# Layer 1's adaLN weights in 24 groups of eight blocks, with slots of their own

## What is computed

```python
cs = jax.nn.silu(c)
for i in range(DEPTH):
    mod = cs @ ada_w[i] + ada_b[i]                      # (9 rows) x 2048 x 12288
    sh1, sc1, g1, sh2, sc2, g2 = jnp.split(mod, N_ADA, axis=-1)
    h = rmsnorm(x, norm_mix_g[i]) * (1.0 + sc1[:, None]) + sh1[:, None]
    ...                                                 # layer 0: retention, layer 1: pooling mixer
    x = x + g1[:, None] * out
    h = rmsnorm(x, norm_ffn_g[i]) * (1.0 + sc2[:, None]) + sh2[:, None]
    x = x + g2[:, None] * swiglu(h, ffn_w_in[i], ffn_w_out[i])
```

## Time and profile before

| | |
|---|---|
| median of three runs | 3528.49 us (3526.47 to 3534.52) |
| the profiled execution, its own time | 3536.41 us |
| its span (first to last instruction) | 3534.6 us |
| TensorE busy | 3344.4 us, 95% |
| weight loads into TensorE (overlap the matmuls) | 3085.7 us, 87% |
| VectorE busy | 1757.5 us, 50% |
| ScalarE busy | 1096.7 us, 31% |
| moved by DMA | 701 MB, mean 198 GB/s |
| mean granted TensorE clock | 0.965 of 2.4 GHz |
| first feed-forward, first weight block to the last output lap | 1363 to 2396 us |
| layer 1's first feed-forward step | 2546 to 2618 us |

### The profile page before, as it was taken

The page is one execution under the profiler, slowest core; times in us unless marked ns, Lnnn a source line. Parts: engine busy times, 40 slices in busy tenths (PEclk is TensorE's granted clock), DMA queues, the critical chain, the costliest instruction groups (busy, mean ns, idle before and its releaser), DMA issues.

```text
span 3534.6 us, 54959 instructions
## 1 busy us (share of the span) xinstructions
PE 3344.4 (95%) x23769; PEld 3085.7 (87%) x23769; DVE 1757.5 (50%) x2696; ACT 1096.7 (31%) x1356; POOL 95.0 (3%) x149
## 2 busy tenths in 40 slices
PE   7799999999999987999999999996699999999997
PEld 3598888988889867999999999996599999999997
DVE  3134473645636475444444444446835555555555
ACT  2232222323223223333332323233333333333333
POOL 0000000000000010000000000001100000000000
PEclk7799999999999998999999999997799999999998
DMA  9775868668686765667666666662264444444442
GB/s 314 250 241 192 273 200 257 211 218 259 205 265 207 226 212 180 219 226 227 226 222 218 217 215 216 219 218 94 74 212 149 150 150 150 151 151 151 149 149 72
DMA packets 627858, 701.12 MB, mean 198 GB/s; under 512 B 21133, under 2 KB 590925, under 8 KB 627289
## 3 DMA queue, kind: packets, MB, share of 16 engines
q1 hardware_dynamic: 606016, 619.26, 54.5%
q0 software_dynamic: 20512, 74.97, 6.6%
q10 hardware_dynamic: 1090, 3.38, 0.3%
HBM read 656.05 MB, written 41.48 MB: 197 GB/s over the span
## 4 chain that ended last, share of the span: by engine, by line
PE 87%; DMA 5%; DVE 5%; ACT 1%; issue 1%; ACTq 0%; POOL 0%; SPq 0%; POOLq 0%; DVEq 0%
PE pair L1323 26%; PE pair L1325 25%; PE pair L1324 25%; PE adab L1339 4%; DMA sb_raw<-in_ada_w 3%; DVE sb_w_lo L819 1%; PE m L1309 1%; DMA sb_o_s<-in_ada_w 1%; DVE sb_silu_g L859 1%; PE m L1534 1%; PE m L1568 1%; DVE sb_big L1134 1%; PE pair L1309 1%; DMA sb_raw<-in_ret_w_in 1%; DMA sb_big<-in_ada_w 1%
## 5 line engine op out<-in xcount | busy, mean ns | idle before, releaser
L819 DVE TENSOR_TENSOR sb_w_lo<-sb_raw,sb_w_hi 128x1024 fp32r<-128x1024 f32 x792 | 965.3, 1223 | 1323.5 <-ACT sb_w_hi L540 1317.3
L540 ACT ACTIVATE sb_w_hi<-sb_raw 128x1024 fp32r<-128x1024 f32 x792 | 838.1, 1059 | 1957.4 <-PE pair L1325 1182.0
L1323 PE MATMUL pair<-sb_h_hi,sb_w_hi 128*128 128x320 f32 x4480 | 1414.6, 316 | 32.0 <-DVE sb_h_lo L1235 15.1
L1325 PE MATMUL pair<-sb_h_hi,sb_w_lo 128*128 128x320 f32 x4480 | 1393.1, 311 | 0.0
L1324 PE MATMUL pair<-sb_h_lo,sb_w_hi 128*128 128x320 f32 x4480 | 1393.0, 311 | 0.0
L1323 PEld LDWEIGHTS pair<-sb_h_hi,sb_w_hi 128*128 128x128 f32 x4480 | 849.0, 190 | 83.2 <-issue 50.0
L1324 PEld LDWEIGHTS pair<-sb_h_lo,sb_w_hi 128*128 128x128 f32 x4480 | 849.1, 190 | 0.0
L1325 PEld LDWEIGHTS pair<-sb_h_hi,sb_w_lo 128*128 128x128 f32 x4480 | 848.2, 189 | 0.0
L1323 PE MATMUL pair<-sb_y_hi,sb_w_hi 128*128 128x320 f32 x1856 | 581.5, 313 | 10.7 <-DVE sb_y_lo L1122 10.7
L1324 PE MATMUL pair<-sb_y_lo,sb_w_hi 128*128 128x320 f32 x1856 | 575.4, 310 | 0.0
L1325 PE MATMUL pair<-sb_y_hi,sb_w_lo 128*128 128x320 f32 x1856 | 575.2, 310 | 0.0
(11 more groups left out here) (212 smaller groups left out, 1489.0 us busy)
## 6 DMA issues: line engine op xcount, KB each, us to landing
sb_raw<-in_ffn_w_in SPq DMA_DIRECT2D x352, 512.0 KB, 3.6
sb_raw<-in_ada_w SPq DMA_DIRECT2D x320, 512.0 KB, 4.7
sb_raw<-in_ret_w_in SPq DMA_DIRECT2D x192, 512.0 KB, 6.0
sb_raw<-in_ffn_w_out SPq DMA_DIRECT2D x176, 512.0 KB, 3.7
sb_big<-in_state_ret POOLq DMA_DIRECT2D x32, 1024.0 KB, 8.0
sb_raw<-in_ret_w_out SPq DMA_DIRECT2D x64, 512.0 KB, 4.1
out_state_ret_sample<-sb_big POOLq DMA_DIRECT2D x32, 1024.0 KB, 5.8
sb_big<-in_ada_w SPq DMA_DIRECT2D x20, 512.0 KB, 7.2
```

Source lines behind the costliest of these rows:

```text
L540: A(w_hi[s][:, :, :], raw[slot][:, :, :], ACT.Copy).then_inc(hi_done, 1)
L819: V.tensor_tensor(w_lo[s][:, :, :], raw[slot][:, :, :], w_hi[s][:, :, :].bitcast(F32), ALU.subtract)\
L1323: MM(out, wh, hi[:, c, :], start=first and k == 0, stop=False)
L1325: ins = MM(out, wl, hi[:, c, :], start=False, stop=last and k == BK - 1)
```

## The change

Layer 1's ada blocks leave the ring. They get nine slots (`v_tok`, `o_s` and seven pieces of `big`, which lie unused during the first feed-forward) and are done in 24 groups of two strips, eight blocks each, at every eleventh weight block of the first feed-forward: group g after its weight block 11g + 6 (`ada_eight`), the fold of both strips one block later (`fold_eight`; both are called after every `gemm` of a lap), ScalarE's copy of 512 columns at its split 11g + 10, ahead of the posts (`copy_eight`), VectorE's add at its split 11g + 11, behind them (`take_eight`). The loads go out on SyncE between the weight loads, block i of group g after the load with number 11g + 4 + i (`load_ff`, `load_eight`), not before number 8 from the third block on. Block b waits for block b - 9 to be used; the third to ninth wait for `h_ready` 8 instead. Layer 1's first step has no ada work any more.

```diff
+FF_FIRST, EIGHT_FROM, EIGHT_EVERY, EIGHTS = H * 32, 6, 11, 24
+EIGHT_SLOTS = 9
...
+def eights_due(gemms, late=0):
+    g, rest = divmod(gemms - FF_FIRST - EIGHT_FROM - late, EIGHT_EVERY)
+    return rest == 0 and 0 <= g < EIGHTS
...
-    halves += [True] * 4 + ([True] * 2 + none + [True] * 2) * (FF_STEPS - 1) + none + none
-    halves += [True] * 4 + none * 3 * (FF_STEPS - 1) + none
+    halves += none * 2 * (1 + 3 * FF_STEPS)
...
+        eight = [t.rearrange("p (k n) -> p k n", k=BK) for t in
+                 [v_tok[:, :, :].rearrange("p c t -> p (c t)"), o_s[:, :, :].rearrange("p c t -> p (c t)")]
+                 + [big[:, 1024 * i:1024 * i + 1024] for i in range(EIGHT_SLOTS - 2)]]
+        eight_sb = k_tok[:, :, :].rearrange("p t n -> p (t n)")
...
+            def load_eight(b):
+                g, i = divmod(b, 8)
+                e = b % EIGHT_SLOTS
+                if b >= EIGHT_SLOTS:
+                    sp.wait_ge(ada_done, 4 * 3 * DC + b - EIGHT_SLOTS + 1)
+                elif b < 2:
+                    sp.wait_ge(pe["F"], H)
+                    sp.wait_ge(state_prompt_out, 16 * H)
+                else:
+                    sp.wait_ge(h_ready, 8)
+                sp.dma_start(eight[e], block_of(a["ada_w"][1], 512 * (i % 4), BN * (2 * g + i // 4))).then_inc(eight_in[e], 16)
+            eights = [max(EIGHT_EVERY * (b // 8) + 4 + b % 8, 8 if b >= 2 else 0) for b in range(8 * EIGHTS)]
+            def load_ff(layer, src):
+                load_block(src)
+                while layer == 0 and eights and C.n["gemm"] - FF_FIRST >= eights[0]:
+                    eights.pop(0)
+                    load_eight(8 * EIGHTS - 1 - len(eights))
...
+            def copy_eight():
+                act.wait_ge(ada_done, C("adas") * 4 + 8)
+                act.wait_ge(ada_folded, C("adas", -ADA0))
+                A(eight_sb, adab[:, :], ACT.Copy).then_inc(ada_copied, 2)
+                C.n["adas"] += 2
...
+                    if eights_due(C.n["gemm"], 4):
+                        copy_eight()
...
+            def take_eight():
+                dve.wait_ge(ada_folded, C("adas", 2 - ADA0))
+                chunk = C("adas", -3 * DC) * 2
+                bias = ada_bT[:, C("adas") * 2:C("adas") * 2 + 4].unsqueeze(2).broadcast_to([P, 4, NC9])
+                src = mbank[C("adas", 0, 2) % 2][:, 0:4 * NC9].rearrange("p (c n) -> p c n", c=4)
+                V.tensor_tensor(mods[1][:, chunk:chunk + 4, :], src, bias, ALU.add).then_inc(mod_dve, 2)
+                C.n["adas"] += 2
...
+                    if eights_due(C.n["gemm"], 5):
+                        take_eight()
...
+            def ada_eight():
+                pe_.wait_ge(ada_copied, C("adas", -ADA0))
+                for i in range(8):
+                    b = C.n["ada"] - 4 * 3 * DC
+                    e, lap = b % EIGHT_SLOTS, b // EIGHT_SLOTS
+                    pe_.wait_ge(eight_in[e], 16 * lap + 16)
+                    for j in range(4):
+                        ins = MM(adab[KPAD * j:KPAD * j + KPAD, BN * (i // 4):BN * (i // 4) + BN], csT[:, 4 * (i % 4) + j, :],
+                                 eight[e][:, j, :], start=i % 4 == 0, stop=i % 4 == 3)
+                    ins.then_inc(ada_done, 1)
+                    C.n["ada"] += 1
+                C.n["adas"] += 2
+            def fold_eight():
+                pe_.wait_ge(ada_copied, C("folds", 2 - ADA0))
+                pe_.wait_ge(mod_dve, C("folds", -2 * H))
+                bank = mbank[C("folds", 0, 2) % 2]
+                for c in range(4):
+                    ins = MM(bank[:, NC9 * c:NC9 * c + NC9], eight_sb[:, P * c:P * c + P], fold, start=True, stop=True)
+                ins.then_inc(ada_folded, 2)
+                C.n["folds"] += 2
+            def eights_beside():
+                if eights_due(C.n["gemm"]):
+                    ada_eight()
+                if eights_due(C.n["gemm"], 1):
+                    fold_eight()
```

More of the change, by code:

```diff
@@ new lines, in _, with feed_forward @@
+            eights = [max(EIGHT_EVERY * (b // 8) + 4 + b % 8, 8 if b >= 2 else 0) for b in range(8 * EIGHTS)]
+            def feed_forward(layer, i, out=True):
+                w1, w2 = a["ffn_w_in"][layer], a["ffn_w_out"][layer]
+                for col in (i * 512, None, i * 512 + DFF):
+                    if col is None and out:
+                        for s in range(8):
+                            load_ff(layer, block_of(w2, i * 512 - 512, BN * s))
+                    elif col is not None:
+                        for n in range(8):
+                            load_ff(layer, block_of(w1, 512 * (n % 4), col + BN * (n // 4)))
@@ L394, in _ @@
+            assert not eights
             for s in range(8):
                 load_block(block_of(a["pool_w"][0, s // 2], 0, BN * (s % 2)))
[L396 to L399, removed]
+            feed_forward(1, 0, out=False)
+            for i in range(1, FF_STEPS):
+                feed_forward(1, i)
             load_k4(a["ffn_w_out"][1], (FF_STEPS - 1) * 512)
@@ L787, in _ @@
             split_ahead()
-            norm(3, GAIN_FFN + DC, mods[1], SH2, ada=True)
-            feed_forward(first=True, ada=True, ahead=AHEAD, end=True)
-            copy_ada()
+            norm(3, GAIN_FFN + DC, mods[1], SH2)
+            feed_forward(first=True, ahead=AHEAD)
             for _ in range(1, FF_STEPS):
@@ L833, in take_mod, with lap @@
                 C.n["adas"] += step
-            def lap(posts, ada=False, pend=False, ahead=0, take=True):
+            def take_eight():
[5 more added lines that the diff above has]
+                C.n["adas"] += 2
+            def lap(posts, ahead=0):
                 for k in range(8):
@@ L1169, in out_between_steps @@
                 split()
-            lap({6: [finish_k]}, take=False)
+            lap({6: [finish_k]})
             lap({3: [finish_q]})
@@ L1284, in _ @@
             split_ahead()
[L1285 to L1288, removed]
+            norm(3, GAIN_FFN + DC, mods[1], SH2, SC2)
+            feed_forward(mods[1], first=True, ahead=AHEAD)
             for _ in range(1, FF_STEPS):
@@ L1366, in lap16 @@
                         gemm(range(4 * k, 4 * k + 4), k == 0, k == 3)
-                        if folds and k == 0 and (pend if j == 0 else ada):
-                            fold_ada()
+                        eights_beside()
                         if ada and k % 2 and j < halves:
@@ L1635, in _, with feed_forward, ff_out @@
             out_lap(h_hi, h_lo)
[L1638 to L1645, removed]
+            def feed_forward(fresh=None):
+                lap16(fresh=fresh)
+                if fresh is None:
+                    ff_out(since=2)
+                lap16()
+            def ff_out(since=0):
                 pe_.wait_ge(pair_free[1], C("strip", -since, 2))
-                lap4(pend=pend)
+                lap4()
             norm(1)
-            feed_forward(fresh=4, ada=True)
+            feed_forward(fresh=4)
             for _ in range(1, FF_STEPS):
-                feed_forward(ada=True)
-            ff_out(pend=True)
+                feed_forward()
+            ff_out()
             norm(2)
```

80 lines of the change are left out of this document (34 added, 46 removed).

## The result

The changed kernel took 3508.42 us (median of five runs, 3506.22 to 3511.62) against 3533.45 for the kernel before, run beside it; the ratio is 0.9930, 95% interval 0.9918 to 0.9941. That is 25 us less, between 21 and 29. Run once more on another chip session it gave 0.9933 (0.9921 to 0.9946). The profiled execution has a span of 3506.5 us where the one before had 3534.6: 28.1 us less, which is also the sum of the prediction. That the two agree to a tenth is chance: 1.2 us of the measured difference lie in the retention part, which the change does not touch.

A forecast was written before the change was run, and what follows sets the result against it. TensorE's own instruction stream was taken to bound the kernel. Savings of 13.2 + 15.3 + 0.6 - 1.0 = 28.1 us take the profiled 3536.4 to 3508.3, and the median of 3528.5 to 3500.4 us; range 3490 to 3514.

The forecast's parts named there:

- What bounds the kernel: First feed-forward, 1363 to 2390 us: the length of TensorE's own instruction stream counts, 1026 us by prices against 1027.0 measured.
- The group of eight: Eight ada blocks in one piece on TensorE cost 3.78 us, where four pairs cost 4.80; bounds 3.44 and 4.80.
- The fold: Fold of two strips, eight records, costs 0.88 us, charged by the record; bounds 0.44 and 0.99.
- First feed-forward, its last lap and the gap before it: Cheaper groups and folds save 13.2 us, the gap before the last output lap 0.6; the first group's wait costs 1.0.
- Layer 1's first step: Removing its eight pairs and four folds saves 15.3 us: 9.7 usual price, 3.9 last pair and fold, 1.7 clock.
- The first group: Its loads stand behind h_ready 8, so TensorE waits between nothing and 2 us for blocks; 1.0 taken.
- Room for the loads: Steady state: the eighth ada block of a group lands three us before TensorE asks for it, at the slower rate.
- the first: Rival: the clock falls to 1.2 GHz at the groups, 24 x 1.7 = 41 us lost, 3541 us; chance 5%.
- the second: Rival: ada blocks come late at the DMA limit, each group waits, 3512 us at 0.5 us a group; chance 11%.
- the third: Rival: grouping saves no switch, each pair in a group pays 1.20 us, 3525 us; chance 4%.

The follow-up runs named there:

- the pairs: Changed kernel with the eight ada blocks of the first 23 groups done as four pairs behind four consecutive weight blocks; ratio to before 0.9988.
- the fours: Changed kernel with 48 groups of four ada blocks, each with its own fold, copy and add; ratio to before 0.9952.
- the doubled groups: Changed kernel with TensorE doing the 32 matmuls of each group twice, on the same blocks; ratio to before 1.0150.
- the loads one later: Changed kernel with each ada load from the second group on issued one weight load later, 3.5 us; ratio to before 0.9937.
- the fold moved alone: Kernel before with only the last fold, its copy and adds moved into the next step's gate lap; ratio to before 0.9987.
- the loads two later: Changed kernel with each ada load from the second group on issued two weight loads later, 7.0 us; ratio to before 1.0048.
- the last group in the wait: Changed kernel with its last group moved from weight block 259 to 256, where TensorE waits for y_lo; 3501.74 us, ratio to before 0.9919.

## Why the prediction was right

- **What bounds the kernel**: right. 15.3 of the 28.1 us come from a stretch in which TensorE was busy throughout before and after. The sum of 1026 us for that stretch met the measured 1027.0 partly by luck: its first 6.1 us ran at 1.2 GHz, which loses 3 us that the sum lacks, and the 88th pair starts only at 2389.85, behind the last weight matmul. The changed kernel starts the stretch the same way (1.2 GHz until 1367.0, 5.2 us), so the difference hardly feels it. It shows in the forecast of some 1015 us up to the last lap's wait, where 1011.4 were measured: the last group lies behind the wait.
- **The group of eight**: 3.78 forecast from four blocks in the opening, 3.79 measured. The pairs, the fours and the doubled groups give the same two numbers, 0.34 us a switch and 0.43 a block.
- **The fold**: 0.88 forecast, 0.88 measured; merging them saves nothing, as the fours show too.
- **First feed-forward, its last lap and the gap before it**: 13.2 + 0.6 - 1.0 = 12.8 us forecast, 15.3 - 3.6 = 11.7 found. The gap before the lap came out at 5.26 us as forecast. The lap's own excess of about 1.2 us is the clock: after the gap it is low for 6.8 us in both kernels, but in the changed one the fall (at 2377.3) comes 1 us before TensorE is back at work and in the kernel before (at 2393.1) 3.5 us before, so that more of that time is spent working at 1.2 GHz, 5.75 us against 3.25. I had not priced that. First the kernel before, then the changed one, then the kernel with the loads one later, whose stream is the same here and whose clock is back after 3.4 us:

```profile
2393.10:2399.90 6.80, 3.25 (x12) 3.25 (x13) 2.65 (x3) 0.74 (x1) 0.00 (x0) 0.50 0.74 244
```

```profile
2377.30:2384.10 6.80, 5.75 (x21) 5.76 (x22) 0.82 (x1) 0.13 (x1) 0.00 (x0) 0.50 0.44 149
```

```profile
2378.50:2381.90 3.40, 2.95 (x11) 2.95 (x12) 0.39 (x1) 0.00 (x0) 0.00 (x0) 0.50 1.02 346
2381.90:2385.30 3.40, 3.40 (x25) 3.40 (x24) 1.11 (x4) 1.06 (x1) 0.00 (x0) 1.00 0.15 52
```
- **Layer 1's first step**: 15.3 forecast and 15.3 found. The run with the fold moved alone supports the split into 9.7, 3.9 and 1.7: where the idle time shrank, the fall of the clock went.
- **The first group**: between nothing and 2 us forecast and 1.0 taken, 0.4 and 0.5 measured, 1.7 in one other run. The bounds were the right ones, the value was 0.5 too high.
- **Room for the loads**: three microseconds forecast at the slower DMA rate; in the trace the eighth blocks land 3.6 to 6.1 us early, and the edge was found between 3.5 and 7.
- **Rivals**: all three fell: the first by the doubled groups, whose 7.2 us of narrow work leave the clock at 1.00; the second by the stretch from 1388.8 us on, in which TensorE is idle nowhere; the third by the pairs, which give the 23 us back, and by the doubled groups' semaphores. The Trainium skill's sentence on transposes (TensorE: Matmul & The Clock Gate, Part 4) does not carry over to narrow matmuls here: the doubled groups' 1.00 shows it.
- **The time itself**: 3500.4 forecast, 3508.4 measured, inside the range of 3490 to 3514. The step that was off is the last one, from the sum to a median. The three runs shown had a median of 3528.5, the five in the result 3533.5, so 5 of the 8 us are the level of the kernel before. The other 3 are the difference of 28.1 between two single profiles to 25.0 between medians, of which 1.2 lie in untouched code; the rest is inside the interval of 21 to 29.

## What to carry to other kernels

Where one engine is busy without a gap, price every small insertion by start-to-start distances around it: the fixed part of a switch (here 0.34 us) is what batching saves, and the part by the piece (0.43 us a block, 0.11 a fold record) stays. Look for the waits that the same engine has anyway, and put the batch there: here it cost nothing, and the clock stayed up behind the wait. Before moving loads later or batches closer, find the edge by shifting them: a delay below the slack was free, and the next step cost more than its waits.

## What the hardware did that I had not expected

- Short waits of TensorE in otherwise dense work are enough to lower its clock. In the kernel with the loads two later, seven groups with an idle gap of 1.87 to 2.91 us, and one with gaps of 0.78 and 2.27, are each followed by 3.4 us at 1.2 GHz; of the 14 with gaps of 0.84 to 1.70 none is. In the kernel before, 2.1 us idle in two pieces did it, and 0.99 us at the same place did not; nor did the 1.36 us behind the last group in the wait.
- How long the clock stays low behind the same wait differs from one execution to the next. Behind the 4.95 us of idle time before the first feed-forward's last output lap it was 6.8 us in both profiles of the changed kernel, in the doubled groups and in the loads two later, and 3.4 us in the pairs, the fours and the loads one later. In the output lap that makes 40.7 us against 39.4 (changed kernel, loads one later), and it is part of the scatter in the table. Why it comes out one way or the other was not looked into.
- The price of work in the array is repeatable to about 0.02 us from group to group, while the untouched retention part began the feed-forward up to 10 us earlier or later from one profile to the next. What varies there was not looked into.
